# Narrow products on two 64-column halves of the array, and heads taken in turn in attention's value products

## The reference

```python
proj = hn @ w_in                                    # (256, 4*1024 + 16)
qkv  = silu(causal_depthwise_conv(proj[..., :3072], conv_w))
beta = sigmoid(proj[..., 4096:4104])                # the "tail": 8 beta
g    = -exp(a_log) * softplus(proj[..., 4104:] + dt_bias)   # and 8 decay columns
q, k = l2_norm(q) * 128**-0.5, l2_norm(k)           # sum of squares over each head's 128 channels
...                                                 # chunked delta rule, w_out, dense SwiGLU
s = einsum('bnqhgd,bnkhd->bnhgqk', q, k_band) + bias   # query chunk of 64, keys of 3 chunks
p = softmax with a sink logit
o = einsum('bnhgqk,bnkhd->bnqhgd', p, v_band)       # the value products
logits = xt @ router_w                              # (256, 8), top 2, gates
...                                                 # per expert: (silu(x @ w_gate) * (x @ w_up)) @ w_down
```

## Time and profile before

| | |
|---|---|
| median of 3 runs | 1544.12 us |
| the profiled execution | 1545.63 us |
| its span (first to last instruction) | 1543.8 us |
| TensorE busy | 1501.1 us, 97% of the span |
| VectorE, ScalarE, GpSimd busy | 1125.6, 898.2, 98.9 us |
| granted TensorE clock, mean | 0.988 |

### The profile page before, as it was taken

The page is one execution under the profiler, slowest core; times in us unless marked ns, Lnnn a source line. Parts: engine busy times, 40 slices in busy tenths (PEclk is TensorE's granted clock), DMA queues, the critical chain, the costliest instruction groups (busy, mean ns, idle before and its releaser), DMA issues.

```text
span 1543.8 us, 22118 instructions
## 1 busy us (share of the span) xinstructions
PE 1501.1 (97%) x8727; PEld 1249.7 (81%) x8727; DVE 1125.6 (73%) x1052; ACT 898.2 (58%) x851; POOL 98.9 (6%) x62
## 2 busy tenths in 40 slices
PE   7999999999989989999999999999999999999997
PEld 6985967999978567888888888888888888888885
DVE  4756355444442449888998998898989898889785
ACT  5630134334423427767777776777777777677674
POOL 2331010000000000000000000000000000000000
PEclk9989999999999979999999999999999999999999
DMA  7521016555462167999999999999999999999992
GB/s 273 199 99 67 9 49 205 179 190 184 150 243 96 55 245 284 381 362 373 395 395 366 393 383 356 379 387 369 395 391 348 393 393 362 374 381 373 380 383 110
DMA packets 194316, 438.01 MB, mean 284 GB/s; under 512 B 5248, under 2 KB 28064, under 8 KB 194144
## 3 DMA queue, kind: packets, MB, share of 16 engines
q1 hardware_dynamic: 189232, 423.64, 74.8%
q0 software_dynamic: 2736, 9.31, 2.4%
q10 hardware_dynamic: 2304, 4.43, 0.8%
HBM read 429.48 MB, written 7.88 MB: 283 GB/s over the span
## 4 chain that ended last, share of the span: by engine, by line
PE 76%; DMA 9%; DVE 6%; ACT 5%; issue 3%; POOL 0%; DVEq 0%; SPq 0%; ACTq 0%
PE bank L1500 19%; PE bank L1502 19%; PE bank L1501 19%; DMA weights<-in_moe_w_gate 6%; DVE weights_lo L1166 3%; PE bank L1850 2%; PE bank L1721 2%; PE bank L1909 2%; PE bank L1535 2%; ACT weights_hi L756 2%; DMA weights<-in_moe_w_down 2%; PE bank L2020 1%; DVE ws L985 1%; DMA weights<-in_moe_w_up 1%; ACT qkv_hi L650 1%
## 5 line engine op out<-in xcount | busy, mean ns | idle before, releaser
L1166 DVE TENSOR_TENSOR weights_lo<-weights,weights_hi 128x2048 fp32r<-128x2048 f32 (+1 forms) x396 | 823.4, 2122 | 144.6 <-ACT weights_hi L756 143.5
L756 ACT ACTIVATE weights_hi<-weights 128x2048 fp32r<-128x2048 f32 (+1 forms) x396 | 685.4, 1781 | 271.5 <-DMA weights<-in_moe_w_up 110.2
L1500 PE MATMUL bank<-weights_hi,expert_x_hi 128*128 128x512 f32 x896 | 355.0, 396 | 1.9 <-DVE expert_x_lo L1379 1.6
L1502 PE MATMUL bank<-weights_hi,expert_x_lo 128*128 128x512 f32 x896 | 349.4, 390 | 0.0
L1501 PE MATMUL bank<-weights_lo,expert_x_hi 128*128 128x512 f32 x896 | 349.2, 390 | 0.0
L1500 PE MATMUL bank<-weights_hi,hidden_hi 128*128 128x512 f32 x528 | 207.5, 393 | 3.1 <-DVE hidden_lo L1204 3.1
L1501 PE MATMUL bank<-weights_lo,hidden_hi 128*128 128x512 f32 x528 | 205.6, 389 | 0.0
L1502 PE MATMUL bank<-weights_hi,hidden_lo 128*128 128x512 f32 x528 | 205.6, 389 | 0.0
L1500 PEld LDWEIGHTS bank<-weights_hi,expert_x_hi 128*128 128x128 f32 x896 | 168.3, 188 | 36.4 <-DVE expert_x_lo L1379 1.2
L1502 PEld LDWEIGHTS bank<-weights_hi,expert_x_lo 128*128 128x128 f32 x896 | 168.3, 188 | 36.4
L1501 PEld LDWEIGHTS bank<-weights_lo,expert_x_hi 128*128 128x128 f32 x896 | 168.4, 188 | 33.4
(11 more groups left out here) (308 smaller groups left out, 1548.3 us busy)
## 6 DMA issues: line engine op xcount, KB each, us to landing
weights<-in_moe_w_down SPq DMA_DIRECT2D x56, 2048.0 KB, 9.7
weights<-in_moe_w_up SPq DMA_DIRECT2D x56, 2048.0 KB, 9.5
weights<-in_moe_w_gate SPq DMA_DIRECT2D x55, 2048.0 KB, 9.6
weights<-in_a_w_in SPq DMA_DIRECT2D x8, 2048.0 KB, 8.8
weights<-in_ffn_w_up SPq DMA_DIRECT2D x11, 1024.0 KB, 5.3
weights<-in_ffn_w_gate SPq DMA_DIRECT2D x11, 1024.0 KB, 5.3
weights<-in_ffn_w_down SPq DMA_DIRECT2D x11, 1024.0 KB, 4.9
weights<-in_a_w_out SPq DMA_DIRECT2D x2, 2048.0 KB, 8.4
```

What stands on the lines that cost most here:

```text
L756: act.activation(hi[:, j * n:(j + 1) * n], slot[k][:, j * n:(j + 1) * n], ACT.Copy).then_inc(w_hi[k], 1)
L1166: dve.tensor_tensor(to[:, c], slot[k][:, c], hi[:, c].bitcast(F32), ALU.subtract).then_inc(w_lo[k], 1)
L1500: pe.matmul(dst, ah, bh, start=start, stop=False, skip_group_check=True)
L1502: return pe.matmul(dst, al, bh, start=False, stop=stop, skip_group_check=True)
```

## The change

Four loops are rewritten on TensorE. The tail, the sums of squares and the router split each 128-column stationary into two halves of 64 columns, the first writing PSUM partitions 0 to 63, the second 64 to 127; the results lie where they lay. In `heads` the loops over the block of keys (`kk`) and over the head of the pair (`hp`) are swapped. No wait, no other engine and no transfer is touched.

```diff
             for t in range(NT):
                 for kt in range(KT):
-                    m = pe.matmul(tail[:, t, :], xt[:, kt, t * P:(t + 1) * P], wtail[:, kt, :],
-                                  start=kt == 0, stop=kt == KT - 1)
+                    for par in range(2):
+                        m = pe.matmul(tail[par * C:par * C + C, t, :], xt[:, kt, t * P + par * C:t * P + par * C + C],
+                                      wtail[:, kt, :], start=kt == 0, stop=kt == KT - 1)
             m.then_inc(s_tail, 1)
...
                     t, hh = divmod(un, H)
-                    m = pe.matmul(bank[4][:, a_ * NU + un:a_ * NU + un + 1], sq[:, a_, hh, t * P:(t + 1) * P],
-                                  K("one"), start=True, stop=True)
+                    for par in range(2):
+                        m = pe.matmul(bank[4][par * C:par * C + C, a_ * NU + un:a_ * NU + un + 1],
+                                      sq[:, a_, hh, t * P + par * C:t * P + par * C + C], K("one"), start=True, stop=True)
             m.then_inc(s_sumsq, 1)
...
                 for j in range(2):
-                    for hp in range(2):
-                        for kk in range(nk):
+                    for kk in range(nk):
+                        for hp in range(2):
                             rows_ = w if kk == nk - 1 else P
                             m = pe.matmul(bank[5][hp * C:hp * C + C, j * T + n * C:j * T + (n + 1) * C],
...
                 for kt in range(KT):
-                    m = pe.matmul(bank[4][:, t * E:(t + 1) * E], xt[:, kt, t * P:(t + 1) * P], router[:, kt, :],
-                                  start=kt == 0, stop=kt == KT - 1)
+                    for par in range(2):
+                        m = pe.matmul(bank[4][par * C:par * C + C, t * E:(t + 1) * E],
+                                      xt[:, kt, t * P + par * C:t * P + par * C + C], router[:, kt, :],
+                                      start=kt == 0, stop=kt == KT - 1)
             m.then_inc(s_log, 1)
```

## The result

The changed kernel takes 1534.8 us, the median of 5 runs (1532.88 to 1539.11); the kernel before took 1544.1 in 5 runs (three of them the ones known before). The ratio of the means is 0.9948, with a 95% interval of 0.9931 to 0.9965: 8.0 us less, 5.4 to 10.7 (the medians differ by 9.3). Run once more on another occasion, in more rounds, it gave 0.9932 (0.9917 to 0.9947), 10.5 us less. The forecast was 1534.0, 10.1 us less.

What follows compares the result with a forecast made beforehand. The prediction took TensorE to bound the kernel, with 76% of the chain, and the 128-column load to fill narrow products' time. Gains 0.9 + 6.2 + 3.0 + 0 = 10.1 us from the median 1544.12 gave 1534.0, range 1530.2 to 1538.2.

Steps and rivals of the forecast that it cites:

- Cost of a half: A 64-column half product: 0.030 us at clock 1.00, 0.057 at 0.50; two halves 0.060 where the whole cost 0.112.
- Part A: The tail's 32 products in halves: `qkv(0)` starts 1.6 us earlier, 0.9 us gained, bounds 0 and 1.2.
- the cap: In the tail's gain: ScalarE's line 669 waits 1.23 us for TensorE and no more; upper bound 1.2 us.
- Part B: The sums of squares in halves: 4.8 us instead of 11.0, 6.2 us gained, bounds 3.3 and 6.7.
- the 4.8 of the sum: Sums of squares: 97 halves before the clock falls at 2.9 us, 1.8 us for 31 more, 0.1 for form changes.
- The cap of 6.7: Behind the sums of squares: tile 19's convolution, then GpSimd's power, keep line 1021 from starting before 96.65; gain at most 6.7 us.
- my signs of being wrong: Halves 0.055 us apart, line 1021 held by GpSimd, or expert layers taking more time than before.
- Part C: Value products, loops of `heads` swapped: 1.0 us in each of groups 0, 2 and 3; 3.0 gained, bounds 1.5 and 4.0.
- the sum's 4 x 0.26: `heads(g, 2)` as 4 runs of 4: 1.03 us if the second head costs nothing, 1.27 otherwise.
- Part D: The router's products in halves: 1.7 us earlier, but ScalarE's gates come behind two casts of expert weights; gain 0.
- The expert layers: Behind the router: they start earlier by what is gained ahead of them, with no fixed instant found that would swallow it.
- The cost of profiling: The profiled execution, 1545.63 us, and the median, 1544.12, were said to differ by it.

Runs made afterwards that it cites:

- e_blocked: The changed kernel, but the sums of squares do all 32 first halves, then all 32 second halves; these products take 10.45 us instead of 4.34.
- p_tail: The kernel before with only the tail's products in halves (line 1494); ratio 1.0001 (0.9991 to 1.001).
- e_block4: The changed kernel, but the sums of squares alternate halves in runs of 8 MATMULs; these products take 4.83 us.
- e_padded: The changed kernel, but `heads(g, 2)` takes 128 rows in its second block of keys too, the added rows zeroed; ratio 0.9953 (0.9936 to 0.997).
- e_gates: The changed kernel, but ScalarE makes the router's gates between the two casts of the expert's weights; 1534.86 us, ratio 0.9943 (0.9928 to 0.9957).
- e_gates_wide: As `e_gates`, but with the router's products whole again; executed once, 11.4 us from merge to the gates.
- e_both: The changed kernel with 128 rows in every block of `heads(g, 2)` and the gates between the two casts; 1531.78 us, ratio 0.9923 (0.9908 to 0.9939).
- p_sumsq: The kernel before with only the sums of squares in halves (line 1569); ratio 0.9959 (0.9945 to 0.9973), 6.3 us less.
- p_router: The kernel before with only the router's products in halves (line 1948); ratio 0.9998 (0.9988 to 1.0008).

## Why the prediction was right, and where it was off

- **Cost of a half.** Taken 0.030 us at 2.4 GHz, 0.057 at 1.2; measured 0.029, and 0.053 in the tail (63 steps from the first to the last MATMUL in 3.33 us). Line 1625 came out as the right row to go by. That line 1600 (0.055) was limited by its 128 moving columns is likely, but no run shows it. `e_blocked` shows that it is the alternation that pays.
- **Part A.** Taken 0.9; 1.0 in the changed kernel's trace, 0.6 in `p_tail`, 0.9 in the mean of all traces. The number is right partly by luck: I took it from TensorE's pace in `qkv(0)`, and what sets line 669 in both traces is ScalarE's own list, the cap. I had put that cap at 1.2 and taken it as fixed, but it moves with the landing of the second weights, on which ScalarE's casts wait.
- **Part B.** Taken 6.2, measured 6.6. The 4.34 us of the products are less than the 4.8 of the sum, mainly since the clock fell 3.2 us after they began, not 2.9. The cap of 6.7 through tile 19's convolution and GpSimd's power was close but did not bind here: the power ended at 89.70 + 5.44 = 95.14, and line 1021 came at 95.39, directly behind the convolution of tile 20, for which ScalarE had waited 3.54 us for TensorE. It binds in the five traces where the slow clock behind the sums lasted only 3.4 us instead of 6.8 (`e_block4`, `e_padded`, `e_gates`, `e_gates_wide`, `e_both`). In these, line 1021 waits for GpSimd and comes 12.6 us after the sums begin, not 12.8. In `e_both`:

```profile
95.79 0.17 DVE L1025 TENSOR_TENSOR sm<-sm 128x16 f32<-128x16 f32 x1 [1.20 <-POOL sm L534]
```

  (Line 1025 of that kernel is line 1021 here.) A line 1021 held by GpSimd was one of my signs of being wrong. There it costs nothing of the forecast: the gain at this cap is 6.9 us, 19.5 less 12.6.
- **Part C.** Taken 3.0, measured 3.15; `heads(g, 2)` takes 1.05 us, which is the sum's 4 x 0.26 with the second head at no cost. Group 1's gain became the wait of 1.07 us, as said.
- **Part D.** 0, as said, and for the reason said.
- **The expert layers** kept their length: 977.7 and 977.8 us from the gather to the end. That they agree to a tenth is luck: over the fourteen traces they take 974.8 to 980.3.
- **The cost of profiling.** I put the 1.5 us between the profiled execution and the median down to it. Nothing shows that: later executions of the kernel before differ by more (next point).
- **What I under-rated** is how much executions differ. I had three runs within 0.7 us; later ones of the kernel before spread from 1538.6 to 1547.3. Two causes show in the traces. One item of the expert loop takes 119.1 us to the tenth, except where a transfer of weights comes late; the changed kernel's chain has `910.63` and `1150.41` as starts of line 1988 two items apart, 239.8 us instead of 238.2, with transfers of weights of 9.9 to 13.4 us in the chain between. The other is the clock.

## What to carry to other kernels

A product with few moving columns costs what the load of its stationary costs. Two halves of 64 columns that alternate, or follow one another in runs of up to 8 MATMULs, load side by side, 0.03 us each where a whole takes 0.11; halves in runs of 64 give nothing at all. Quarters came at 0.009 us each but lost more to a pause of 4.6 us in a stream of 256, so they want a trial of their own. Ahead of such an edit look for what stands behind the place on the *other* engines: here ScalarE's list held back all of the router's gain, and a softmax one group's of four. Where two orders are equally good, keep products with the same number of rows together.

## What I had not expected of the hardware

**The clock may fall behind a wait that a gain has opened (not shown).** In `e_gates` the clock fell in `values(2)`, some 2 us behind the wait of 1.07 us that the swap had opened. Windows of TensorE (window, length, busy, granted clock, DMA share, GB/s), and `heads(2, 2)` and `heads(2, 3)` there:

```profile
500.00:506.90 6.90, 5.67 (x85) 1.00 0.39 159
507.60:514.20 6.60, 6.60 (x47) 0.50 0.00 0
514.50:520.00 5.50, 5.50 (x14) 1.00 0.00 0
509.11 2.76 PE L1901 MATMUL bank<-ws 128*64 128x64 f32 x32
```

2.76 us for what takes 1.74, and 3.0 us lost by the end of merge (73.6 us from scores(0), for 70.65). It fell so in 3 of the 10 traces that have the swap (`e_gates`, `e_gates_wide`, `e_padded`) and in none of the 4 that don't. The other seven have the wait too and keep 2.4 GHz there. So that the wait has to do with it is not shown, and no run tried to close it.

**The clock alone moves stretches that no edit touches.** From line 1021 to scores(0) I measured 372.9 us in `p_sumsq`, 374.4 in the changed kernel and 375.9 in `e_gates`; in these stretches the clock was at 1.2 GHz not at all, once and twice, for 3.4 us each time. All fourteen traces fall into these three groups: 372.7 to 373.3 us in four, 374.2 to 374.4 in six, 375.8 to 376.0 in four. So such a stretch costs about 1.5 us. Between the sums of squares and line 1021 the kernel before took 19.5 us in its own trace, and the same code 17.9 in those of `p_tail` and `p_router`, where the slow clock lasted 10.2 us instead of 13.7. With the halves it is 12.6 to 12.8. Part B's gain is therefore anything from 5.1 to 6.9 us, by chance of the execution.
